# Combination weights spread as two fp32r parts, and a reordered end of the expert loop, in a three-layer transformer kernel

## The reference

```python
def hier_moe(h, wr_g, br_g, wr_e, br_e, w_gate, w_up, w_down):
    ...
    combine = jnp.sum(jax.nn.one_hot(expert_id, N_EXPERTS, dtype=f32) * top_w[..., None], axis=1)
    hid = jax.nn.silu(jnp.einsum('td,edf->etf', t, w_gate)) * jnp.einsum('td,edf->etf', t, w_up)
    hid = hid * combine.T[:, :, None].astype(hid.dtype)
    out = jnp.einsum('etf,efd->td', hid, w_down)
    return out.reshape(B, S, D)

...
    h = h + hier_moe(rms_norm_2(h, norm2_g[l]), ...)
    return rms_norm_2(h, final_norm_g)
```

## Time and profile before

| | |
|---|---|
| median of 3 runs | 1939.43 us (1939.19 to 1945.26) |
| profiled execution | 1944.3 us |
| its span, first to last instruction | 1942.5 us |
| granted TensorE clock, mean | 0.961 |
| TensorE matmuls busy | 1816.0 us, 93% |
| VectorE busy | 1174.5 us, 60% |
| ScalarE busy | 750.6 us, 39% |
| DMA | 310.74 MB, 160 GB/s on average |

### The profile page before, as it was taken

The page is one execution under the profiler, slowest core; times in us unless marked ns, Lnnn a source line. Parts: engine busy times, 40 slices in busy tenths (PEclk is TensorE's granted clock), DMA queues, the critical chain, the costliest instruction groups (busy, mean ns, idle before and its releaser), DMA issues.

```text
span 1942.5 us, 32746 instructions
## 1 busy us (share of the span) xinstructions
PE 1816.0 (93%) x13650; PEld 1705.9 (88%) x13650; DVE 1174.5 (60%) x1550; ACT 750.6 (39%) x851; POOL 10.9 (1%) x24
## 2 busy tenths in 40 slices
PE   6899669999998999999999999989999999999996
PEld 6889447899987768999989988889899999999996
DVE  6677883677767575455544667645365555555654
ACT  1222353454333324653323554423334334343332
POOL 0000000000000000000100000000000000000000
PEclk8899788999999999999989999998899999999998
DMA  8255421366763212455634432332255455554541
GB/s 315 93 197 194 152 94 58 113 247 243 265 248 130 87 66 87 155 191 210 245 127 152 174 131 93 116 140 89 98 184 184 183 183 184 181 186 177 190 174 63
DMA packets 43580, 310.74 MB, mean 160 GB/s; under 512 B 5239, under 2 KB 5624, under 8 KB 6952
## 3 DMA queue, kind: packets, MB, share of 16 engines
q1 hardware_dynamic: 41904, 302.80, 42.9%
q0 software_dynamic: 1200, 5.58, 0.9%
q10 hardware_dynamic: 392, 1.12, 0.2%
HBM read 308.44 MB, written 1.05 MB: 159 GB/s over the span
## 4 chain that ended last, share of the span: by engine, by line
PE 80%; DVE 13%; ACT 3%; issue 2%; DMA 1%; ACTq 0%; SPq 0%; DVEq 0%
PE ps L526 22%; PE ps L528 22%; PE ps L527 22%; DVE macc L1526 3%; DVE wlo L1514 2%; PE ps L599 2%; ACT whi L1091 2%; PE ps L645 1%; PE ps L581 1%; PE ps L583 1%; PE ps L582 1%; PE ps L632 1%; DVE y L1569 1%; DVE small L1670 1%; PE ps L893 1%
## 5 line engine op out<-in xcount | busy, mean ns | idle before, releaser
L1514 DVE TENSOR_TENSOR wlo<-raw,whi 128x2048 fp32r<-128x2048 f32 x237 | 542.4, 2291 | 403.2 <-ACT whi L1091 401.9
L526 PE MATMUL ps<-uhi,whi 128*128 128x256 f32 x2496 | 716.4, 287 | 16.7 <-DVE ulo L1556 6.0
L527 PE MATMUL ps<-uhi,wlo 128*128 128x256 f32 x2496 | 709.0, 284 | 0.0
L528 PE MATMUL ps<-ulo,whi 128*128 128x256 f32 x2496 | 708.6, 284 | 0.0
L1091 ACT ACTIVATE whi<-raw 128x2048 fp32r<-128x2048 f32 x237 | 452.3, 1911 | 382.4 <-PE ps L528 362.2
L526 PEld LDWEIGHTS ps<-uhi,whi 128*128 128x128 f32 x2496 | 481.7, 193 | 27.3 <-issue 19.4
L527 PEld LDWEIGHTS ps<-uhi,wlo 128*128 128x128 f32 x2496 | 482.0, 193 | 0.9 <-issue 0.7
L528 PEld LDWEIGHTS ps<-ulo,whi 128*128 128x128 f32 x2496 | 481.6, 193 | 0.0
L526 PE MATMUL ps<-ehi,whi 128*128 128x256 f32 x512 | 144.7, 283 | 5.7 <-DVE elo L2136 5.7
L526 PE MATMUL ps<-hid_hi,whi 128*128 128x256 f32 x512 | 144.9, 283 | 1.6 <-ACTq L1252 1.6
L527 PE MATMUL ps<-ehi,wlo 128*128 128x256 f32 x512 | 144.4, 282 | 0.0
(11 more groups left out here) (354 smaller groups left out, 2057.2 us busy)
## 6 DMA issues: line engine op xcount, KB each, us to landing
raw<-weights_in SPq DMA_DIRECT2D x277, 1024.0 KB, 4.8
mstart<-mod_start_in SPq DMA_DIRECT2D x4, 2048.0 KB, 19.8
w1c<-cmp_w_in POOLq DMA_DIRECT2D x1, 2048.0 KB, 15.3
h<-x_in SPq DMA_DIRECT2D x1, 1024.0 KB, 7.9
ctx<-ctx_in SPq DMA_DIRECT2D x1, 1024.0 KB, 18.6
y<-decay_in ACTq DMA_DIRECT2D x1, 1024.0 KB, 4.7
out<-y SPq DMA_DIRECT2D x4, 256.0 KB, 2.5
conb<-const_b_in POOLq DMA_DIRECT2D x1, 656.0 KB, 7.0
```

The lines of the kernel that those rows point to most:

```text
L526: mm(o, w0, x0, start=first, stop=False, **kw)
L527: mm(o, w1, x0, start=False, stop=False, **kw)
L528: return mm(o, w0, x1, start=False, stop=last, **kw)
L1514: tt(wlo[:, sl, :], raw[:, sl, :], f32(whi[:, sl, :]), ALU.subtract).then_inc(s("lo_ready"), 1)
```

## The change

- **Spread.** `cbt` becomes two fp32r parts, and `pick`, an fp32r copy of the identity made by ScalarE, is the stationary operand. ScalarE writes the high part, VectorE subtracts for the low part, after its four weight splits. Each expert's spread is two fp32r matmuls (high, low) into the same place. ScalarE evicts the even pairs, VectorE the odd ones.
- **Loop.** On both engines the split of `hmid` goes ahead of `split(i + 5 + RING)`.
- **After the loop.** TensorE runs 7 filler matmuls once all `silu` results have left PSUM, then the two down chunks. ScalarE no longer waits for the last two chunks.
- **Final norm.** Adding, squaring and summing go in four pieces. The first piece's sum is put into the middle of the last chunk.
- **Tables.** `root_ahead` takes the root of a one-column constant, at three places: before `head_roots`, before the split of `merged`, and before the final squares.

In the diff the tables of turns and the buffers come first, then the programs of TensorE, ScalarE and VectorE.

```diff
-                    ("mlp1", 4), ("mix_in", 4), ("moe_in", 4), ("final", 2)],
+                    ("mlp1", 4), ("mix_in", 4), ("moe_in", 4), ("final", 4)],
...
-        "h": [(t, 2 if t == "moe" else 4) for t in ("post0", "mlp0", "post1", "mlp1", "mixed", "moe")],
+        "h": [(t, 4) for t in ("post0", "mlp0", "post1", "mlp1", "mixed", "moe")],
...
-            cbt = alloc(st, "cbt", [T])
+            cbt = alloc(st, "cbt", [2, T], F32R)
+            pick = alloc(st, "pick", [EXPERTS], F32R)
...
+            def sum_part(tag, bank, c, src=sq):
+                _, part = cuts(tag, "squares")[c]
+                pe.wait_ge(*nth(tag, "squares", c + 1))
+                for k in range(part.start, part.stop):
+                    ins = mm(ps[:, bank, 0:T], ones, src[:, k, :], start=k == 0, stop=k == KT - 1)
+                if part.stop == KT:
+                    ins.then_inc(s("sumsq"), 1)
...
-            pe.wait_ge(s("combine_copied"), 1)
+            pe.wait_ge(s("combine_hi"), 1)
+            pe.wait_ge(s("combine_lo"), 1)
             for e in range(EXPERTS):
                 if e >= 8 and e % 2 == 0:
-                    pe.wait_ge(s("comb_stored"), (e - 8) // 2 + 1)
-                ins = mm(ps[:, 4 + (e // 2) % 4, (e % 2) * T:(e % 2 + 1) * T], ident[0:EXPERTS, e:e + 1].to_broadcast([EXPERTS, P]),
-                         cbt[0:EXPERTS, :], start=True, stop=True)
+                    pe.wait_ge(s("comb_by_dve" if e // 2 % 2 else "comb_by_act"), (e - 8) // 4 + 1)
+                o, one = ps[:, 4 + (e // 2) % 4, (e % 2) * T:(e % 2 + 1) * T], pick[0:EXPERTS, e:e + 1].to_broadcast([EXPERTS, P])
+                mm(o, one, cbt[0:EXPERTS, 0, :], start=True, stop=False)
+                ins = mm(o, one, cbt[0:EXPERTS, 1, :], start=False, stop=True)
...
-            for j in range(2):
-                down_rows(N_CHUNKS - 2 + j, j)
-            sum_squares("final", 0)
+            pe.wait_ge(s("moe_silu"), 2 * EXPERTS)
+            idle_work(0, 7)
+            down_rows(N_CHUNKS - 2, 0)
+            down_rows(N_CHUNKS - 1, 1, between=lambda: sum_part("final", 0, 0))
+            for c in range(1, 4):
+                sum_part("final", 0, c)
...
+            def root_ahead():
+
+                fn(small[:, 60:61], eps, ACT.Sqrt)
...
+            fn(pick[0:EXPERTS, :], ident[0:EXPERTS, 0:EXPERTS], ACT.Copy)
             act.wait_ge(s("combine_turned"), 1)
-            fn(cbt[0:EXPERTS, :], ps[0:EXPERTS, 5, 0:T], ACT.Copy).then_inc(s("combine_copied"), 1)
-            for e in range(EXPERTS // 2):
+            fn(cbt[0:EXPERTS, 0, :], ps[0:EXPERTS, 5, 0:T], ACT.Copy).then_inc(s("combine_hi"), 1)
+            for e in range(0, EXPERTS // 2, 2):
                 act.wait_ge(s("comb_spread"), e + 1)
...
-                for j in range(2):
-                    product(i + 4 + j, n, 6)
-                    split(i + 4 + j + RING, n, 6)
+                product(i + 4, n, 6)
+                split(i + 4 + RING, n, 6)
+                product(i + 5, n, 6)
                 for j in range(2):
                     expert_high(j, n)
-            for j in range(2):
-                product(N_CHUNKS - 2 + j)
+                split(i + 5 + RING, n, 6)
+            root_ahead()
             next_squares("final", "moe")
...
-            dve.wait_ge(s("comb_stored"), EXPERTS // 2)
+            dve.wait_ge(s("combine_hi"), 1)
+            tt(cbt[0:EXPERTS, 1, :], ps[0:EXPERTS, 5, 0:T], f32(cbt[0:EXPERTS, 0, :]), ALU.subtract).then_inc(s("combine_lo"), 1)
+            for e in range(1, EXPERTS // 2, 2):
+                dve.wait_ge(s("comb_spread"), e + 1)
+                nc.vector.tensor_copy(comb[:, 2 * e:2 * e + 2, :], halves(ps[:, 4 + e % 4, :])).then_inc(s("comb_by_dve"), 1)
...
-                for j in range(2):
-                    weighted(i + 4 + j, j, n)
-                    split(i + 4 + j + RING, n, 6)
+                weighted(i + 4, 0, n)
+                split(i + 4 + RING, n, 6)
+                weighted(i + 5, 1, n)
                 for j in range(2):
                     expert_low(j, n)
+                split(i + 5 + RING, n, 6)
...
-            for j in range(2):
-                add_rows(N_CHUNKS - 2 + j, j, last=True)
+            for c, a in cuts("moe", "h"):
+                dve.wait_ge(s("chunk_used"), N_CHUNKS - 1 + c // 2)
+                tt(h[:, a, :], h[:, a, :], halves(ps[:, 4 + c, :]), ALU.add).then_inc(s("h"), 1)
```

More of the change, by code:

```diff
@@ L593, in modulation @@
                 used(ins)
-            def sum_squares(tag, bank, src=sq):
[L596 to L600, removed]
+            def sum_part(tag, bank, c, src=sq):
[5 more added lines that the diff above has]
+                    ins.then_inc(s("sumsq"), 1)
+            def sum_squares(tag, bank, src=sq):
+                for c, _ in cuts(tag, "squares"):
+                    sum_part(tag, bank, c, src)
             def filter_layer(j):
@@ L1039, in up_rows, with down_rows @@
                 used(tiles(i, lambda m, _: ps[:, bank, m * T:(m + 1) * T], [u_parts]))
-            def down_rows(i, j, n=None):
+            def down_rows(i, j, n=None, between=None):
                 if n is None:
@@ L1048, in down_rows @@
                 weights_ready(i, n, 6)
-                used(tiles(i, lambda m, _: ps[:, 4 + 2 * j + m // 2, (m % 2) * T:(m % 2 + 1) * T], [(ehi, elo)], kts=4, width=4))
+                used(tiles(i, lambda m, _: ps[:, 4 + 2 * j + m // 2, (m % 2) * T:(m % 2 + 1) * T], [(ehi, elo)], kts=4, width=4,
+                           between=between))
             for j in range(4):
@@ L1474, in _ @@
                 split(I_MOE + 2 + j + RING)
+            fn(pick[0:EXPERTS, :], ident[0:EXPERTS, 0:EXPERTS], ACT.Copy)
             act.wait_ge(s("combine_turned"), 1)
-            fn(cbt[0:EXPERTS, :], ps[0:EXPERTS, 5, 0:T], ACT.Copy).then_inc(s("combine_copied"), 1)
-            for e in range(EXPERTS // 2):
+            fn(cbt[0:EXPERTS, 0, :], ps[0:EXPERTS, 5, 0:T], ACT.Copy).then_inc(s("combine_hi"), 1)
+            for e in range(0, EXPERTS // 2, 2):
                 act.wait_ge(s("comb_spread"), e + 1)
-                fn(comb[:, 2 * e:2 * e + 2, :], halves(ps[:, 4 + e % 4, :]), ACT.Copy).then_inc(s("comb_stored"), 1)
+                fn(comb[:, 2 * e:2 * e + 2, :], halves(ps[:, 4 + e % 4, :]), ACT.Copy).then_inc(s("comb_by_act"), 1)
             for j in range(2):
@@ L2136, in expert_low, with add_rows @@
                 tt(elo[:, a, :], hmid[:, a, :], f32(ehi[:, a, :]), ALU.subtract).then_inc(s("moe_hid"), 1)
-            def add_rows(i, j, n=None, last=False):
+            def add_rows(i, j, n=None):
                 dve.wait_ge(s("chunk_used"), up(i + 1, n, 6))
@@ L2141, in add_rows @@
                 tt(h[:, a, :], h[:, a, :], ps[:, 4 + 2 * j:6 + 2 * j, :].rearrange("p b (m t) -> p (b m) t", m=2), ALU.add)\
-                    .then_inc(s("h" if last else "moe_free"), 1)
+                    .then_inc(s("moe_free"), 1)
             for j in range(4):
                 split(I_MOE + j + RING)
-            dve.wait_ge(s("comb_stored"), EXPERTS // 2)
+            dve.wait_ge(s("combine_hi"), 1)
[3 more added lines that the diff above has]
+                nc.vector.tensor_copy(comb[:, 2 * e:2 * e + 2, :], halves(ps[:, 4 + e % 4, :])).then_inc(s("comb_by_dve"), 1)
+            dve.wait_ge(s("comb_by_act"), EXPERTS // 4)
+            dve.wait_ge(s("comb_by_dve"), EXPERTS // 4)
             for j in range(2):
```

## The result

| | before | after |
|---|---|---|
| median, 7 runs each in the same rounds | 1944.12 us (1939.19 to 1945.26) | 1934.94 us (1933.28 to 1938.23) |
| ratio, 95% interval | | 0.9958 (0.9942 to 0.9973) |
| profiled execution, its span | 1944.3, 1942.5 us | 1934.02, 1932.1 us |
| from the first transpose of `cb` to the end of the span | 1942.5 - 1376.68 = 565.82 us | 1932.1 - 1374.33 = 557.77 us |

What follows compares the result with a forecast made beforehand. TensorE was taken to bound the kernel (80% of the chain), fully busy in the expert loop, with gains only at its two ends. 4.2 + 3.7 + 0.6 = 8.5 us off the 1939.43 median gave 1931.0 us, range 1927.5 to 1935.5.

Steps and rivals of the forecast that it cites:

- The base: Time the gain was subtracted from: the 1939.43 us median of three runs, giving 1931.0; from the profiled 1944.3, 1935.8.
- The sum: Whole gain at the expert loop's two ends: 4.2 + 3.7 + 0.6 = 8.5 us.
- Part 1: Spread of combination weights ahead of the loop: 32 fp32r matmuls replace 16 fp32 ones, ending 4.2 us earlier.
- part 2: Loop's end: activations split before the last weight split, fillers hold the clock; TensorE resumes earlier, 3.6 to 3.7 us gained.
- The clock in the spread: New spread ahead of the loop assumed at half clock throughout, 0.213 us per matmul, with about 4.1 us of half-clock expert matmuls following.
- rival B: Denser new spread counts as work for the clock, full clock returns within it; 11.4 us in all, 1928.0; chance 0.10.
- The slack in the loop: Inside the expert loop the weight split starts 2.1 us later against slack of 4.9, so 15 experts cost nothing.
- Part 3: Final norm in pieces, one of four sums moved into the middle of the last chunk; gains 0.6 us.
- Part 4: Early table loads by `root_ahead`: gain 0, since loads already lie ahead of the waits; ends 0 and 0.2 us.
- C: Spread's 16-row weight loads not hidden, about 0.33 us per instruction; 4.7 us in all, 1934.7; chance 0.08.
- D: Fillers after the loop run at half clock, 6.5 us, and become the wait; 5.3 us in all, 1934.1; chance 0.05.
- E: Each spread fp32r matmul costs a whole fp32 one, 0.84 us; kernel slower, 1951.0; chance 0.03.

Runs made afterwards that it cites:

- e8: The kernel before, unchanged, profiled once more; 1941.64 us.
- e6: The changed kernel with 128-row operands (zeros above the 16) in the spread, parts made where the change makes them; one run, 1930.14 us.
- e4: The changed kernel with both `cbt` parts made ahead of the fourth weight split and 128-row zero-padded spread operands; median 1926.67 us, ratio to before 0.9908.
- e5: The changed kernel with both `cbt` parts made ahead of the fourth weight split, operands still of 16 rows; one run, 1924.77 us.
- e3: The changed kernel without the seven filler matmuls after the loop; one run, 1937.47 us.
- e9: The changed kernel with the first of the final norm's four sums behind the last chunk instead of inside it; one run, 1932.47 us.
- e10: The changed kernel without the three early roots (`root_ahead`); one run, 1935.16 us.
- e11: The changed kernel with early `cbt` parts, 128-row spread operands and the first sum behind the last chunk; median 1924.02 us, ratio to before 0.9910.
- e7: The kernel before with only the loop's order changed, the split of `hmid` ahead of the weight split on both engines; one run, 1939.28 us.

## Why the prediction was right and wrong

**The base, wrong.** The step that failed is "from the median I get 1931.0". 1939.43 was the middle one of three runs, 1939.43, 1945.26 and 1939.19, and the profiled execution at 1944.3 stood beside them: two of four near 1939, two near 1945. I wrote of it as "4.9 above the median" and did not let the range hold it. Over 22 runs of before the median was 1944.21, over 9 on another chip 1941.28; and the runs fill the space between the two, 1938.05 to 1948.04 us in twenty of the 22. e8 shows where the spread lies: ahead of the router, in stretches that the change leaves alone. In the fourteen profiles of this study the first transpose of `cb` falls between 1371.2 and 1378.1 us, in kernels that do the same work up to there but for a small copy or root. With the profiled 1944.3 as the base, as the sum was worked out at first (1935.8), the figure of 1936.0 from 7 runs is met; a range on the median had to reach some 5 us further up. The subtraction itself is off by a little: 1939.43 - 8.5 is 1930.9.

**The sum, 8.05 instead of 8.5, nearer than its terms.** Part 1 fell short by 0.8 us and part 2 gave 0.3 to 0.4 more, so the total came out closer than part 1 did, and that is luck.

**Part 1, mechanism right, 3.4 instead of 4.2.** The wait for VectorE's split was met (4.96 us after the transposes, 4.9 forecast), so was 0.213 per matmul at half clock. The spread took 7.09 rather than 6.8, as its first record and the change to the next kind cost some 0.15 each. And the slow expert matmuls behind it lasted 5.1 us (1386.38 to 1391.45), not the 4.2 of before: four more of them, 0.4 us, where the sum had left 0.6 either way.

**The clock in the spread, right.** It stayed at 0.50 through all 32 (windows 1379.20 to 1386.20), so rival B fell. The Trainium skill (TensorE: Matmul & The Clock Gate, "Why this matters for your kernels") would have had it return under sustained work. The trace of this spread does not agree, and the runs add the condition under which it did: with 128 rows the clock returned in the spread (e6) or stayed (e4), with 16 it fell in the midst of work (e5).

**Part 2, right, 4.0 against 3.6 to 3.7.** From the last up product to the adds of the first down chunk 12.89 us became 8.90. TensorE resumed 2.85 us after the product instead of 5.53, so 2.7 us earlier and not 2.1: the loop's exit cost the fillers nothing, where I had allowed 0.2, and they started sooner and took 3.14, not 3.3. The 13 slow matmuls were worth the other 1.3 us and not 1.5: they start 0.213 us apart, not 0.236, but for the first distance of 0.39 us, which at the full clock is still 0.23. The second miss takes back part of the first. The slack in the loop, worked out as 4.9 us against a delay of 2.1, held: 510.03 or 510.04 in the twelve profiles without e4's spread, of either order. That the fillers are needed was right, and the reason that I gave for the clock's staying up, that it was at 0.97 through the old gap, was weak: in e3 it was gone after 3.03 us.

**Part 3, right, 0.6.** 4.61 - 3.99. It is made of 1.47 gained behind the last chunk and 0.86 paid within it; e9 shows that the payment buys nothing.

**Part 4, right, 0.** e10.

**Rivals C, D and E** fell by the same lines: 0.21 us from one spread record to the next, fillers of 3.18 us at clock 1.00. The decision of sign, faster, with 8.05 us against a forecast 8.5, came out as forecast.

## What to carry to other kernels

Forecast a difference from one profile, but before turning it into a time ask which of the shown runs the profile belongs to; where three runs and a profile lie 6 us apart, the range must span them. Ahead of a short chain between engines, put its small operations before the long periodic ones in each engine's queue: here that alone was worth 6.0 us more (e5, one profile), where the cheaper matmuls had brought 3.4. Where the clock matters, try small matmuls with full 128-row operands padded with zeros: here they were worth 3.3 us alone (e6) and 2.9 on top of the early parts (e4 against e5). Cut work into pieces only as finely as the waits need it.

## What the hardware showed unexpectedly

- During back-to-back fp32r matmuls with 16-row operands TensorE's clock fell from 1.00 to 0.50 (e5), and 13.45 us of fp32 ones with 16 rows in the kernel before did not bring it back (the row below, columns as there, is their end); the same fp32r matmuls with 128 rows kept it (e4, e11) or had it back within the spread (e6). The time per fp32r instruction is the same for 16 and 128 rows, 0.21 us at half clock and 0.12 at full.

```profile
1388.00:1392.60 4.60, 4.60 (x12) 3.10 (x11) 0.00 (x0) 1.32 (x3) 0.00 (x0) 0.50 0.01 4
```

- A gap of 3.0 us was enough for the clock to be at 0.50 at resumption, and its return took 13 matmuls in one execution and 27 in another (e7, e3), while in the gap of 5.66 us before it was still granted for most of the time (mean 0.97 in 1910.50 to 1916.00), and 13 were slow behind it.
- Executions of the unchanged kernel on one chip differed by 10 us (1938.05 to 1948.04 us, in twenty of 22 runs). Where profiles were compared, 3.0 us of such a difference stood ahead of the transposes; its largest piece was 3.3 us in a stretch with one- and two-column matmuls whose mean clock was 0.68 in one and 0.61 in the other, and hardly any in the dense loop: 510.04 us in eleven profiles, 510.03 in one, 509.78 in the two with e4's spread.
